# A transformer kernel on one core: the first weight chunk of each dense stage is split in four pieces among the last row blocks

## The chip, the core and the metric

The kernel runs on one NeuronCore of a Trainium2 chip. The core has a matrix engine (TensorE), three engines for elementwise work (VectorE, ScalarE, GpSimd), and SyncE, whose queue issues DMAs. Each engine runs its own list of instructions in order, and they meet at semaphores: an engine waits until a semaphore has reached a number, and finished instructions raise it. The metric is the device time of one execution in microseconds (us), as the median of several runs; lower is better.

## The reference

The program is two transformer blocks over 512 tokens of width 1024, in float32. The first has a mixer (mLSTM heads and a gated MLP), cross attention to 256 memory rows and a mixture of 32 experts; the second, run twice, has a token mixer with four branches and another mixture of experts. What matters here are the dense products in between. Cut to these:

```python
z = h @ w_in                                             # mixer: 1024 -> 3088 columns
x = x + jnp.concatenate([y_mlstm, y_gmlp], -1) @ w_out    # its output projection
q = h @ w_q;  kv = hm @ w_kv                              # cross attention
x = x + o @ w_o
z = x @ w_in                                             # token mixer, per layer
merged @ w_o                                             # its output projection, per layer
```

## The kernel before

Every dense product goes through `dense` (line 86). Its inputs are the activations, turned so that the 1024 features lie on the partitions (`hT`, 8 row blocks of 128 features by 512 tokens), and weight chunks of 256 columns or so (8 row blocks by 256 columns, 1 MB). To keep float32 accuracy at the fast rate, each operand is held as two float32r parts: HI is the rounded value, LO what is left. A product of one row block is three matmuls, HI x HI, HI x LO and LO x HI (`PARTS`), so one output item of `dense` is 8 x 3 = 24 matmuls into one PSUM bank.

A chunk is split in two steps. `high` (line 143, the copy on 147) casts the whole chunk to HI on ScalarE once its DMA has landed; `low` (line 161, line 164) subtracts that from the raw chunk on VectorE. A chunk has 2048 columns per partition, so these are long instructions. TensorE (lines 127 to 139) waits for `low_ready` of the item's chunk, then runs its 24 matmuls on line 137. Two split chunks are held, and two or three raw ones (`raw_ring`); SyncE loads chunk after chunk on line 124.

`before` is the helper that makes `hT` inside the same stage. `TurnSplit` (line 229): TensorE turns four 128x128 tiles into each of the eight PSUM banks (line 246), ScalarE writes HI of each row block (line 253), VectorE writes LO (line 261, or line 263 where a gain is applied). `Split` (line 267) does the same from SBUF without TensorE (lines 281 and 287). All three engines do all of `before` first and only then chunk 0:

```python
before.pe(pe)
pe.wait_ge(before.low_ready, before.n)     # all eight row blocks
...
before.act(act)                            # ScalarE: eight row blocks, then
high(0)                                    #   the whole of chunk 0
...
before.dve(dve)                            # VectorE: eight row blocks, then
low(0)
```

Eight stages call `dense` with a `before`. Four start with items of 512 columns, where the weights are the stationary operand (`by_feature`): mixw (the mixer's input, with a gain, `raw_ring` 2), xaw (cross attention, with a gain), t0w and t1w (the token mixer's input, layer 0 and 1). Four are output projections through `project_onto` (line 1526), with items of 256 columns (`by_token`): mixo, xao, t0o and t1o; of these t0o and t1o use `Split`, the others `TurnSplit`. Chunk 0 has two items in the first four and four in the projections. In mixw, t0w and t1w VectorE also has convolution taps as side work, behind the items of chunks 1 and later. Each stage ends in a clear of its semaphores and a barrier of all engines (lines 53 and 54).

Of the kernel before, what the change touches and what calls it, by code (L numbers as in the profile page):

```python
# [11 lines left out]
HI, LO = 0, 1  # L12
I32 = mybir.dt.int32
U32 = mybir.dt.uint32
ACT = mybir.ActivationFunctionType
# [65 lines left out]


WIDTH = 256


def dense(nc, name, k, chunks, items, raw_ring=3, side=None, before=None):

    ps = k["ps"]
    widest = max(c.shape[2] for c in chunks)
    deepest = max(c.shape[1] for c in chunks)
    last_item = {it.chunk: i for i, it in enumerate(items)}
    nth, counts = [], {"act": 0, "dve": 0}
    for it in items:
        counts[it.engine] += 1
        nth.append(counts[it.engine])
    with Stage(nc, name) as st:  # L100
        raw = st.sb("raw", [P, raw_ring, deepest, widest])
        w = st.sb("w", [P, 2, 2, deepest, widest], F32R)
        landed = [st.sem(f"weights_landed{i}") for i in range(raw_ring)]
        high_ready = st.sem("high_ready")
        low_ready = st.sem("low_ready")
        bank_full = st.sem("bank_full")
        emptied = {"act": st.sem("emptied_by_act"), "dve": st.sem("emptied_by_dve")}

        def raw_of(c):
            return raw[:, c % raw_ring, 0:chunks[c].shape[1], 0:chunks[c].shape[2]]  # L110

        def part_of(c, part):
            return w[:, c % 2, part, 0:chunks[c].shape[1], 0:chunks[c].shape[2]]

        if before is not None:
            before.begin(st)

        with nc.Block() as block:
            @block.sync
            def _(sp):  # L120
                for c, dram in enumerate(chunks):
                    if c >= raw_ring:
                        sp.wait_ge(low_ready, c - raw_ring + 1)
                    sp.dma_start(raw_of(c), dram).then_inc(landed[c % raw_ring], 16)

            @block.tensor
            def _(pe):
                if before is not None:
                    before.pe(pe)
                    pe.wait_ge(before.low_ready, before.n)  # L130
                for i, it in enumerate(items):
                    pe.wait_ge(low_ready, it.chunk + 1)
                    if i >= 8:
                        pe.wait_ge(emptied[items[i - 8].engine], nth[i - 8])
                    pairs = it.operands(w[:, it.chunk % 2])
                    for j, (stationary, moving) in enumerate(pairs):
                        last = nc.tensor.matmul(ps[0:it.rows, i % 8, 0:it.n], stationary, moving,
                                                start=j == 0, stop=j == len(pairs) - 1)
                    last.then_inc(bank_full, 1)

            @block.scalar
            def _(act):
                def high(c):
                    act.wait_ge(landed[c % raw_ring], 16 * (c // raw_ring + 1))
                    if c >= 2:
                        act.wait_ge(bank_full, last_item[c - 2] + 1)
                    nc.scalar.copy(part_of(c, HI), raw_of(c)).then_inc(high_ready, 1)

                if before is not None:
                    before.act(act)  # L150
                high(0)
                for c in range(len(chunks)):
                    if c + 1 < len(chunks):
                        high(c + 1)
                    for i, it in enumerate(items):
                        if it.chunk == c and it.engine == "act":
                            act.wait_ge(bank_full, i + 1)
                            it.out(nc.scalar, ps[0:it.rows, i % 8, 0:it.n]).then_inc(emptied["act"], 1)

            @block.vector  # L160
            def _(dve):
                def low(c):
                    dve.wait_ge(high_ready, c + 1)
                    nc.vector.tensor_tensor(part_of(c, LO), raw_of(c), part_of(c, HI), ALU.subtract).then_inc(low_ready, 1)

                if before is not None:
                    before.dve(dve)
                low(0)
                for c in range(len(chunks)):
                    if c + 1 < len(chunks):  # L170
                        low(c + 1)
                    for i, it in enumerate(items):
                        if it.chunk == c and it.engine == "dve":
                            dve.wait_ge(bank_full, i + 1)
                            it.out(nc.vector, ps[0:it.rows, i % 8, 0:it.n]).then_inc(emptied["dve"], 1)
                    if side is not None:
                        side(dve, c, emptied)


def chunk_of(w_dram, a, b):  # L180
    return w_dram.rearrange("(c p) n -> p c n", p=P)[:, :, a:b]
# [3 lines left out]
PARTS = ((HI, HI), (HI, LO), (LO, HI))  # L185
# [43 lines left out]
class TurnSplit:  # L229
# [16 lines left out]
                last = self.nc.tensor.transpose(self.bank(c)[:, t * P:(t + 1) * P], self.src(t, c), self.k["ident"][:])  # L246
            last.then_inc(self.full, 1)

    def act(self, act):
        for c in range(self.n):  # L250
            act.wait_ge(self.full, c + 1)
            scale = 1.0 if self.factor is None else self.factor[:, c:c + 1]
            self.nc.scalar.activation(self.dst[:, HI, c, :], self.bank(c), ACT.Identity, scale=scale).then_inc(self.high_ready, 1)

    def dve(self, dve):
        vec = self.nc.vector
        for c in range(self.n):
            dve.wait_ge(self.high_ready, c + 1)
            low, high = self.dst[:, LO, c, :], self.dst[:, HI, c, :]
            if self.factor is None:  # L260
                vec.tensor_tensor(low, self.bank(c), high, ALU.subtract).then_inc(self.low_ready, 1)
            else:
                vec.scalar_tensor_tensor(low, self.bank(c), self.factor[:, c:c + 1], high, ALU.mult,
                                         ALU.subtract).then_inc(self.low_ready, 1)


class Split:
# [8 lines left out]
    def pe(self, pe):  # L276
        pass

    def act(self, act):
        for c in range(self.n):  # L280
            self.nc.scalar.activation(self.dst[:, HI, c, :], self.src[:, c, :], ACT.Identity,
                                      scale=self.factor).then_inc(self.high_ready, 1)

    def dve(self, dve):
        for c in range(self.n):
            dve.wait_ge(self.high_ready, c + 1)
            self.nc.vector.scalar_tensor_tensor(self.dst[:, LO, c, :], self.src[:, c, :], self.factor,
                                                self.dst[:, HI, c, :], ALU.mult, ALU.subtract).then_inc(self.low_ready, 1)


def turn_split(nc, name, k, tiles, src, dst, n, factor=None):

    turned = TurnSplit(nc, k, tiles, src, dst, n, factor)
    with Stage(nc, name) as st:
        turned.begin(st)
        with nc.Block() as block:
            @block.tensor
            def _(pe):
                turned.pe(pe)

            @block.scalar
            def _(act):
                turned.act(act)

            @block.vector
            def _(dve):
                turned.dve(dve)


def plain(nc, out, gain=None):  # L310
# [1040 lines left out]
def mixer_one(nc, k, x, col, i):  # L1351
# [3 lines left out]
    with Stage(nc, "mix") as sx:  # L1355
# [5 lines left out]
        with Stage(nc, "mixa") as sa:  # L1361
# [6 lines left out]

            spans = [(a, a + WIDTH) for a in range(0, 1536, WIDTH)] + [(1536, 1800), (1800, 2064)]
            spans += [(a, a + WIDTH) for a in range(2064, 3088, WIDTH)]  # L1370
            chunks = [chunk_of(w, a, b) for a, b in spans]
# [5 lines left out]
            for c in range(2):  # L1377
                cs = slice(c * WIDTH, (c + 1) * WIDTH)
                for t in range(TT):
                    items.append(by_token(4 + c, hT, t, 0, WIDTH, "dve", plain(nc, v[:, t, cs])))  # L1380
            def output_gates(t, a):
# [474 lines left out]
class GatedBranches:  # L1856
# [78 lines left out]
    def high(self, act, u):  # L1935
        act.wait_ge(self.landed[u % self.RAW], 32 * (u // self.RAW + 1))
        if u >= self.SPLIT:
            act.wait_ge(self.proj_full, u - self.SPLIT + 1)
        self.nc.scalar.copy(self.w[:, u % self.SPLIT, HI], self.raw[:, u % self.RAW]).then_inc(self.high_ready, 1)

    def low(self, dve, u):
        dve.wait_ge(self.high_ready, u + 1)
        self.nc.vector.tensor_tensor(self.w[:, u % self.SPLIT, LO], self.raw[:, u % self.RAW],  # L1943
                                     self.w[:, u % self.SPLIT, HI], ALU.subtract).then_inc(self.low_ready, 1)
# [264 lines left out]
```

## Time and profile before

| | |
|---|---|
| three runs | 3113.94, 3120.40 and 3122.73 us, median 3120.4 |
| profiled execution | 3114.51 us, span in the profile 3112.7 us |
| TensorE matmuls | busy 2482.1 us, 80% of the span |
| TensorE weight loads | 1949.6 us, 63% |
| VectorE | 1284.4 us, 41% |
| ScalarE | 881.6 us, 28% |
| GpSimd | 406.1 us, 13% |
| DMA | 565.77 MB, 182 GB/s on average |
| TensorE's mean granted clock | 0.89 |

The shares are averages over stages with quite different limits: the expert stages stream their weights at up to 414 GB/s, while the dense stages move little and are full of matmuls. A dense stage has to be read by itself, in order of time. Times in the rows below are microseconds from the span's start; PE is the matmul side of TensorE and PEld its weight loads, DVE is VectorE, ACT ScalarE, SPq the issuing queue of SyncE. A row of a timeline gives start, length, engine, line and operation, the output and input tiles, how many instructions were merged, and in brackets how long the engine idled before and who ended it.

### The profile page before, as it was taken

The page shows a single profiled execution, that of the slowest core. Times are in us where ns is not written, and L with a number is a line of the kernel's source. Part 1 is how long each engine was busy: PE and PEld are TensorE (multiplying, and loading weights), DVE is VectorE, ACT ScalarE, POOL GpSimd, SP SyncE. Part 2 cuts the span into 40 slices and gives each one's busy share as a digit, 9 for nine tenths or more (in the row PEclk, how much of TensorE's full clock was granted, in tenths as well). Part 3 has the DMA queues.
Part 4 walks back from the last instruction along what each step waited for, and adds up shares of the span by engine and source line. Part 5 has one row for each costly group of instructions (what it writes and reads, how often), then busy time and mean ns, then how long its engine had stood idle before and what let it go on. Part 6 is the DMA issues. An engine that isn't in the chain of part 4 may idle for free. (4 is left out here: it accounts for less than half of the span.)

```text
span 3112.7 us, 50456 instructions
## 1 busy us (share of the span) xinstructions
PE 2482.1 (80%) x18120; PEld 1949.6 (63%) x18121; DVE 1284.4 (41%) x2666; ACT 881.6 (28%) x1612; POOL 406.1 (13%) x716
## 2 busy tenths in 40 slices
PE   4975798868888886969899669983959989849882
PEld 3964678844444445847677657762848667747661
DVE  3437345232111115634653434335644744343334
ACT  2233234111111112144532213322233632213221
POOL 0000000022111210000000124432000000024333
PEclk9988899879999997979999869996979999959996
DMA  3200242389999954122121378994212212179993
GB/s 114 93 1 1 68 135 75 158 322 404 407 414 410 390 239 138 41 68 60 43 68 43 121 286 339 384 367 135 69 35 68 60 51 68 55 288 346 378 393 136
DMA packets 209256, 565.77 MB, mean 182 GB/s; under 512 B 26550, under 2 KB 170550, under 8 KB 184544
## 3 DMA queue, kind: packets, MB, share of 16 engines
q1 hardware_dynamic: 191056, 538.71, 46.7%
q0 software_dynamic: 18064, 25.23, 2.5%
q8 instruction: 87, 1.43, 0.2%
q14 instruction: 49, 0.40, 0.0%
HBM read 560.44 MB, written 36.18 MB: 192 GB/s over the span
## 5 line engine op out<-in xcount | busy, mean ns | idle before, releaser
L1020 PEld LDWEIGHTS ps<-r_gate_up,e_xT 128*64 128x64 f32 x2272 | 267.0, 144 | 92.3 <-issue 88.8
L1020 PE MATMUL ps<-m_gate_up,e_xT 128*64 128x256 f32 x1088 | 269.7, 411 | 61.9 <-DMA m_gate_up<-in_w_gate_up 48.0
L1020 PE MATMUL ps<-r_gate_up,e_xT 128*64 128x128 f32 x2272 | 279.1, 284 | 43.0 <-DMA r_gate_up<-in_w_exp_gate_up 28.5
L1022 PE MATMUL ps<-r_gate_up,e_xT 128*64 128x128 f32 x2272 | 279.3, 284 | 0.0
L1022 PE MATMUL ps<-m_gate_up,e_xT 128*64 128x256 f32 x1088 | 269.8, 411 | 0.0
L1020 PEld LDWEIGHTS ps<-m_gate_up,e_xT 128*64 128x64 f32 x1088 | 159.8, 149 | 174.2 <-issue 110.3
L1022 PEld LDWEIGHTS ps<-r_gate_up,e_xT 128*64 128x64 f32 x2272 | 267.0, 144 | 0.0
L1174 DVE TENSOR_TENSOR e_hid<-e_silu,ps 64x128 f32<-64x128 f32 (+1 forms) x210 | 70.1, 335 | 472.7 <-ACT e_silu L1062 467.9
L1062 ACT ACTIVATE e_silu<-ps 64x128 f32<-64x128 f32 (+1 forms) x210 | 63.8, 304 | 641.8 <-PE ps L1022 641.8
L455 POOL TENSOR_TENSOR all_x<-all_x,ln_rows 128x1024 f32<-128x1024 f32 x16 | 48.2, 3038 | 1263.7 <-DVE all_x L448 1263.7
L1921 PE MATMUL ps<-t_hT,t0a_t0g_w 128*128 128x512 f32 x768 | 199.4, 411 | 4.6 <-DVE t0a_t0g_w L1943 2.4
L1921 PE MATMUL ps<-t_hT,t1a_t1g_w 128*128 128x512 f32 x768 | 199.2, 411 | 4.6 <-DVE t1a_t1g_w L1943 2.4
L1180 DVE TENSOR_SCALAR e_y<-ps 128x512 f32 x105 | 72.6, 692 | 248.9 <-PE ps L1037 213.3
L1921 PEld LDWEIGHTS ps<-t_hT,t0a_t0g_w 128*128 128x128 f32 x768 | 145.5, 194 | 45.8 <-issue 10.3
L1921 PEld LDWEIGHTS ps<-t_hT,t1a_t1g_w 128*128 128x128 f32 x768 | 145.3, 194 | 45.7 <-issue 10.3
L1062 ACT ACT_TABLE_LOAD x105 | 134.7, 1283 | 124.0 <-issue 114.2
L1022 PEld LDWEIGHTS ps<-m_gate_up,e_xT 128*64 128x64 f32 x1088 | 159.8, 149 | 0.0
L1037 PE MATMUL ps<-r_down,e_hidT 128*64 128x512 f32 x568 | 137.5, 605 | 0.0
L1218 POOL COPY e_choicecur<-e_choicecol 128x1 uint32 x106 | 52.3, 493 | 588.5 <-DVE e_y L1180 588.5
L1213 POOL DMA_INDIRECT e_landing<-e_dram_rows,e_tokcur x115 | 117.0, 1017 | 59.5 <-issue 59.5
L1037 PE MATMUL ps<-m_down,e_hidT 128*64 128x512 f32 x544 | 124.2, 598 | 0.0
L1221 POOL DMA_INDIRECT e_dram_y<-e_y,e_choicecur x106 | 110.4, 1041 | 56.4 <-issue 56.0
(605 smaller groups left out, 4740.1 us busy)
## 6 DMA issues: line engine op xcount, KB each, us to landing
m_gate_up<-in_w_gate_up SPq DMA_DIRECT2D x32, 4096.0 KB, 38.2
r_gate_up<-in_w_exp_gate_up SPq DMA_DIRECT2D x64, 2048.0 KB, 33.8
m_down<-in_w_down SPq DMA_DIRECT2D x32, 2048.0 KB, 37.9
r_down<-in_w_exp_down SPq DMA_DIRECT2D x64, 1024.0 KB, 34.7
t0a_t0g_raw<-in_w_in SPq DMA_DIRECT2D x32, 512.0 KB, 3.8
t1a_t1g_raw<-in_w_in SPq DMA_DIRECT2D x32, 512.0 KB, 3.8
mixw_raw<-in_w_in SPq DMA_DIRECT2D x10, 1024.0 KB, 5.4
xaw_raw<-in_w_kv_x SPq DMA_DIRECT2D x8, 1024.0 KB, 5.3
```

Of the source, the lines that this page charges most:

```text
L455: nc.gpsimd.tensor_tensor(x[:, t, :], x[:, t, :], rows[:, 1], ALU.add).then_inc(shifted, 1)
L1020: nc.tensor.matmul(ps_gu[q][0:SLOTS], xT[:, c, :], ring.gu[:, s, 0, c, span], start=c == 0, stop=c == DC - 1)
L1022: last = nc.tensor.matmul(ps_gu[q][SLOTS:P], xT[:, c, :], ring.gu[:, s, 1, c, span], start=c == 0, stop=c == DC - 1)
L1037: last = nc.tensor.matmul(ps_y[h * SLOTS:(h + 1) * SLOTS], hidT[:, f, :], ring.wd[:, s, f, h * 512:(h + 1) * 512], start=f == 0, stop=f == ...
L1062: nc.scalar.activation(silu[SLOTS:P, q], ps_gu[q][0:SLOTS], ACT.Silu).then_inc(silu_ready, 1)
L1174: vec.tensor_tensor(hid[SLOTS:P, q], silu[SLOTS:P, q], ps_gu[q][SLOTS:P], ALU.mult).then_inc(hid_ready, 1)
L1180: vec.tensor_scalar(y[:, bass.ds(g % 2, 1)].rearrange("p one d -> p (one d)"), ps_y, 1.0, None, ALU.mult).then_inc(y_copied, 1)
L1213: nc.gpsimd.indirect_dma_start(landing[:, p], None, rows_dram, bass.IndirectOffsetOnAxis(tokcur[p][:], 0), bounds_check=S - 1, oob_is_err= ...
L1218: nc.gpsimd.tensor_copy(choicecur[p][:], choicecol[:, bass.ds(n, 1)]).then_inc(choicecur_ready, 1)
L1221: nc.gpsimd.indirect_dma_start(y_dram, bass.IndirectOffsetOnAxis(choicecur[p][:], 0), y[:, p], None, bounds_check=4 * S - 1, oob_is_err=Fa ...
L1921: last = nc.tensor.matmul(ps[:, 6, :], w[:, p, q, :], self.hT[:, r, q, :], start=q == 0 and p == r, stop=q == DC - 1 and p == LO)
```

## The change

For stages with a `before`, chunk 0 is split in `FIRST` = 4 pieces of two row blocks (512 columns per partition). ScalarE writes HI of row blocks 0 to 4, waits for chunk 0's landing, casts piece 0, then writes block 5, piece 1, block 6, piece 2, block 7, piece 3. VectorE follows in the same order with the LO parts. Pieces have semaphores of their own, `first_high_ready` and `first_low_ready`, and `low_ready` now counts from chunk 1 on. On TensorE the wait for all eight row blocks is gone; inside item 0, ahead of the three matmuls of row block q, stands a wait for row block q's LO and, for every second q, one for the piece. Item 1 and later ones of chunk 0 wait for all four pieces. The helpers' loops over row blocks (`act`, `dve`) become one call for each block (`high`, `low`), which `turn_split` now loops over itself. Nothing that is computed changes.

```diff
+FIRST = 4
@@ dense
+    first = FIRST if before is not None else 1
+    step = chunks[0].shape[1] // first
+        first_high_ready = st.sem("first_high_ready")
+        first_low_ready = st.sem("first_low_ready")
+        def wait_low(engine, c):
+            if c == 0:
+                engine.wait_ge(first_low_ready, first)
+            else:
+                engine.wait_ge(low_ready, c)
@@ SyncE
-                        sp.wait_ge(low_ready, c - raw_ring + 1)
+                        wait_low(sp, c - raw_ring)
@@ TensorE
-                    pe.wait_ge(before.low_ready, before.n)
-                    pe.wait_ge(low_ready, it.chunk + 1)
+                    if i > 0 or before is None:
+                        wait_low(pe, it.chunk)
                     for j, (stationary, moving) in enumerate(pairs):
+                        if i == 0 and before is not None and j % len(PARTS) == 0:
+                            q = j // len(PARTS)
+                            pe.wait_ge(before.low_ready, q + 1)
+                            if q % step == 0:
+                                pe.wait_ge(first_low_ready, q // step + 1)
@@ ScalarE
+                def first_high(n):
+                    if n == 0:
+                        act.wait_ge(landed[0], 16)
+                    span = slice(n * step, (n + 1) * step)
+                    nc.scalar.copy(part_of(0, HI)[:, span], raw_of(0)[:, span]).then_inc(first_high_ready, 1)
-                    before.act(act)
-                high(0)
+                    for c in range(before.n):
+                        before.high(act, c)
+                        if c >= before.n - first:
+                            first_high(c - before.n + first)
+                else:
+                    first_high(0)
@@ VectorE
+                def first_low(n):
+                    dve.wait_ge(first_high_ready, n + 1)
+                    span = slice(n * step, (n + 1) * step)
+                    nc.vector.tensor_tensor(part_of(0, LO)[:, span], raw_of(0)[:, span], part_of(0, HI)[:, span],
+                                            ALU.subtract).then_inc(first_low_ready, 1)
-                    before.dve(dve)
-                low(0)
+                    for c in range(before.n):
+                        before.low(dve, c)
+                        if c >= before.n - first:
+                            first_low(c - before.n + first)
+                else:
+                    first_low(0)
```

## Rows read from the trace of the kernel before

**Rows 1.** Line 164 asked by source: who waited for it (us, times)
```profile
  PE ps L137: 56.8, 8
```

**Rows 2.** Timeline, opening of mixw
```profile
35.60 13.60 SPq L124 DMA_DIRECT2D mixw_raw<-in_w_in  x4
...
35.64 5.70 PE L246 MATMUL ps<-all_ident,mix_y 128*128 128x128 f32 x32 [35.64 <-PEq L54]
...
37.48 6.03 DVE L263 SCALAR_TENSOR_TENSOR mix_hT<-ps,all_columns,mix_hT 128x512 fp32r<-128x512 f32 x8 [2.58 <-ACT mix_hT L253]
...
39.32 3.17 ACT L253 ACTIVATE mix_hT<-ps,all_columns 128x512 fp32r<-128x512 f32 x5 [0.17 <-PE ps L246]
...
46.75 5.43 PE L137 MATMUL ps<-mix_hT,mixw_w 128*128 128x512 f32 x16 [5.41 <-DVE mixw_w L164]
```

**Rows 3.** Timeline, opening of t0o
```profile
1712.69 4.27 ACT L281 ACTIVATE t_hT<-t_merged 128x512 fp32r<-128x512 f32 x8 [2.93 <-PEq L54]
1713.36 4.91 DVE L287 SCALAR_TENSOR_TENSOR t_hT<-t_merged,t_hT 128x512 fp32r<-128x512 f32 x8 [1.41 <-ACT t_hT L281]
1717.84 1.90 ACT L147 CAST t0o_w<-t0o_raw 128x2048 fp32r<-128x2048 f32 x1 [0.88 <-DMA t0o_raw<-in_w_o]
1719.77 2.29 DVE L164 TENSOR_TENSOR t0o_w<-t0o_raw,t0o_w 128x2048 fp32r<-128x2048 f32 x1 [1.51 <-ACT t0o_w L147]
...
1722.21 5.96 PE L137 MATMUL ps<-t0o_w,t_hT 128*128 128x256 f32 x34 [11.79 <-DVE t0o_w L164]
```

**Rows 4.** DMA issues, chunk 0 of four stages: issue, queue, count, size, us to landing
```profile
mixw_raw<-in_w_in SPq DMA_DIRECT2D x1, 1024.0 KB, 6.0
...
xaw_raw<-in_w_q_x SPq DMA_DIRECT2D x1, 1024.0 KB, 5.1
...
t0w_raw<-in_w_in SPq DMA_DIRECT2D x1, 1024.0 KB, 5.2
...
t1w_raw<-in_w_in SPq DMA_DIRECT2D x1, 1024.0 KB, 5.3
```

**Rows 5.** Timeline, TensorE's transposes and first products in xaw, t0w and t1w
```profile
394.11 5.66 PE L246 MATMUL ps<-all_ident,xa_h 128*128 128x128 f32 x32 [1.75 <-PEq L54]
...
405.18 2.05 PE L137 MATMUL ps<-xa_hT,xaw_w 128*128 128x512 f32 x4 [5.41 <-DVE xaw_w L164]
...
1191.46 6.33 PE L246 MATMUL ps<-all_ident,all_x 128*128 128x128 f32 x32 [32.84 <-PEq L54]
...
1202.73 3.75 PE L137 MATMUL ps<-t_hT,t0w_w 128*128 128x512 f32 x8 [4.94 <-DVE t0w_w L164]
...
2155.57 5.57 PE L246 MATMUL ps<-all_ident,all_x 128*128 128x128 f32 x32 [43.85 <-PEq L54]
...
2166.19 4.12 PE L137 MATMUL ps<-t_hT,t1w_w 128*128 128x512 f32 x10 [5.05 <-DVE t1w_w L164]
```

**Rows 6.** Groups by line and form: count | busy, mean ns | idle before, releaser
```profile
L137 PE MATMUL ps<-t0o_w,t_hT 128*128 128x256 f32 x384 | 48.0, 289 | 11.8 <-DVE t0o_w L164 11.8
...
L137 PE MATMUL ps<-mix_hT,mixw_w 128*128 128x512 f32 x192 | 46.2, 403 | 5.4 <-DVE mixw_w L164 5.4
```

**Rows 7.** Windows, first 10 us of products; after the five engines, PEclk, DMA share, GB/s
```profile
46.75:56.75 10.00, 10.00 (x37) 8.06 (x38) 2.79 (x4) 0.00 (x0) 0.00 (x0) 0.84 0.65 211
...
405.18:415.18 10.00, 10.00 (x37) 8.15 (x38) 2.75 (x2) 0.00 (x0) 0.00 (x0) 0.84 0.68 211
...
1202.73:1212.73 10.00, 10.00 (x35) 7.97 (x36) 2.75 (x2) 0.00 (x0) 0.00 (x0) 0.78 0.58 170
...
2166.19:2176.19 10.00, 10.00 (x37) 8.00 (x38) 2.75 (x2) 0.00 (x0) 0.00 (x0) 0.83 0.58 172
```

**Rows 8.** Timeline and windows around xao's transposes (end 535.60) and product (541.87)
```profile
531.91 3.69 PE L246 MATMUL ps<-all_ident,xa_h 128*128 128x128 f32 x32 [1.50 <-PEq L54]
...
529.00:531.91 2.91, 1.42 (x8) 0.94 (x6) 1.29 (x4) 0.00 (x1) 0.00 (x0) 1.00 0.00 0
...
535.60:538.94 3.34, 0.00 (x0) 0.00 (x0) 2.48 (x5) 2.43 (x4) 0.00 (x0) 0.88 1.10 352
```

More of the change, by code:

```diff
@@ L161, in _ @@
             def _(dve):
+                def first_low(n):
[3 more added lines that the diff above has]
+                                            ALU.subtract).then_inc(first_low_ready, 1)
                 def low(c):
-                    dve.wait_ge(high_ready, c + 1)
+                    dve.wait_ge(high_ready, c)
                     nc.vector.tensor_tensor(part_of(c, LO), raw_of(c), part_of(c, HI), ALU.subtract).then_inc(low_ready, 1)
                 if before is not None:
-                    before.dve(dve)
-                low(0)
+                    for c in range(before.n):
[4 more added lines that the diff above has]
+                    first_low(0)
                 for c in range(len(chunks)):
@@ L247, in pe, with high, low @@
             last.then_inc(self.full, 1)
[L249 to L255, printed above, removed]
-        vec = self.nc.vector
[L257 to L264, printed above, removed]
+    def high(self, act, c):
+        act.wait_ge(self.full, c + 1)
+        scale = 1.0 if self.factor is None else self.factor[:, c:c + 1]
+        self.nc.scalar.activation(self.dst[:, HI, c, :], self.bank(c), ACT.Identity, scale=scale).then_inc(self.high_ready, 1)
+    def low(self, dve, c):
+        vec = self.nc.vector
+        dve.wait_ge(self.high_ready, c + 1)
+        low, high = self.dst[:, LO, c, :], self.dst[:, HI, c, :]
+        if self.factor is None:
+            vec.tensor_tensor(low, self.bank(c), high, ALU.subtract).then_inc(self.low_ready, 1)
+        else:
+            vec.scalar_tensor_tensor(low, self.bank(c), self.factor[:, c:c + 1], high, ALU.mult,
+                                     ALU.subtract).then_inc(self.low_ready, 1)
 class Split:
@@ L277, in pe, with high, low @@
         pass
[L279 to L288, printed above, removed]
+    def high(self, act, c):
+        self.nc.scalar.activation(self.dst[:, HI, c, :], self.src[:, c, :], ACT.Identity,
+                                  scale=self.factor).then_inc(self.high_ready, 1)
+    def low(self, dve, c):
+        dve.wait_ge(self.high_ready, c + 1)
+        self.nc.vector.scalar_tensor_tensor(self.dst[:, LO, c, :], self.src[:, c, :], self.factor,
+                                            self.dst[:, HI, c, :], ALU.mult, ALU.subtract).then_inc(self.low_ready, 1)
 def turn_split(nc, name, k, tiles, src, dst, n, factor=None):
@@ L302, in _ @@
             def _(act):
-                turned.act(act)
+                for c in range(n):
+                    turned.high(act, c)
             @block.vector
             def _(dve):
-                turned.dve(dve)
+                for c in range(n):
+                    turned.low(dve, c)
 def plain(nc, out, gain=None):
```

## The prediction, made before the changed kernel was run

> **What bounds the kernel now.** I read the page first, for which engine is busy, and then, because the change lives only in `dense`, the waits that line 137 (the products) has there. In the whole run those products wait eight times for line 164, the float32 remainder of a weight chunk, once in each of the eight dense stages, for 56.8 us together [rows 1]. No later chunk is waited for in this way, so behind its first product each stage runs at TensorE's pace, and whatever brings product 25 (the second item) forward brings the end of the stage forward. So I read the opening of the stages in order of time: who is late there?
>
> In mixw, one of the four stages with 512-column products, the transposes end at 41.34, ScalarE's row blocks at 42.49, VectorE's at 43.51, and the first product starts only at 46.75 [rows 2]. Between lies the whole of chunk 0: cast and then subtraction, one behind the other. In t0o, one of the four output projections (256 columns), ScalarE is done with its blocks at 1716.96 and then idles 0.88 us for chunk 0's landing; cast 1.90, subtraction 2.29, product at 1722.21 [rows 3]. The serial chain is landing (or last block), 1.90, 2.29, 0.15.
>
> **The change, part by part.**
>
> *Splitting.* One cast of 2048 columns becomes four of 512. For ScalarE the nearest row is the same width from SBUF in t0o: 0.61 for one, and eight in 4.27, so one each 0.52 us; for VectorE 0.69, eight in 4.91, one each 0.60 [rows 3]. Four pieces cost about 2.2 us against 1.90 and 2.5 against 2.29. From below: 0.48 and 0.57 a piece, the exact quarter; from above 0.69, the longest 512-column row of ScalarE [rows 2], and 0.75 on VectorE. I take 0.60 and 0.62. This is 0.2 to 0.3 us per stage and engine, and it lies beside products, see below.
>
> *Order.* ScalarE now does blocks 0 to 4, waits for chunk 0, then piece 0, block 5, piece 1, block 6, piece 2, block 7, piece 3; VectorE follows in the same order. The wait for the landing thus moves ahead of three row blocks, and queued behind it on ScalarE are those blocks, behind them VectorE's remainders, and TensorE. Landing after issue is 6.0, 5.1, 5.2 and 5.3 us in mixw, xaw, t0w and t1w [rows 4]. Block 4's cast in mixw ends about 40.8 (the second of five from 39.32 [rows 2]), so ScalarE stands 0.8 us; in t0o block 4 ends at 1715.4 and it stands 2.4 us until 1717.84 [rows 3]. That delays blocks 5 to 7, yet not the first product, which now needs only row block 0 and piece 0.
>
> *First product.* It comes at landing + 0.60 + 0.03 + 0.69 + 0.15 = landing + 1.47. mixw: 35.60 + 6.0 + 1.47 = 43.07 against 46.75, 3.7 us earlier. xaw: 394.07 + 5.1 + 1.47, with 0.1 for VectorE's block 4 still running, 400.75 against 405.18, 4.4. t0w: 1191.41 + 5.2 + 1.47 = 1198.1 against 1202.73, 4.6. t1w: 2155.53 + 5.3 + 1.47 = 2162.3 against 2166.19, 3.9 [rows 2, 4, 5] (the issue is 0.04 to 0.05 before the first transpose). Sum 16.6. t0o: 1717.84 + 1.47 = 1719.3 against 1722.21, 2.9 [rows 3]; mixo, xao and t1o have the same chain from landing to product (a landing wait, then 1.90, 2.29), so four times 2.9 = 11.7. Together 28.3 us.
>
> *Do the products keep up, or do they now wait for pieces?* VectorE gives a piece and a block each 0.60 + 0.62 = 1.22 us (1.3 in mixw and xaw, whose blocks take 0.66 to 0.75 [rows 2]). Six products use one piece and two blocks. The 192 wide products of mixw take 46.2 us, 0.24 each, so six take 1.4 at full clock: TensorE stays the slower one, and the shift passes whole to the second item. Narrow ones take 48.0/384 = 0.125 [rows 6], six 0.75 at full clock and twice that, 1.5, at half. Those stages begin at half clock (below), so there too TensorE paces. If they ran at full clock they would be held by the last piece: first product + 3 x 1.22 + 0.15 + 0.75, 4.6 us for the item, no longer than they need when they warm up on the way. Last piece lands about 0.7 us later than the last subtraction did; chunk 1 behind it is ready 1 us later, and is needed no sooner than 48 wide or 96 narrow products after the start, 11 us: hidden.
>
> *Waits.* Twelve waits inside item 0 (eight for blocks, four for pieces). The trace shows only what an unsatisfied one costs, 0.15 us from VectorE's end to the product [rows 3], and that one was there before. I take 0 for the others, since they are fulfilled when TensorE comes to them; the other end is 0.15 at each of seven later boundaries, 8 us over eight stages. Two more semaphores per stage are in a clear that stands between barriers; no row of mine prices it, between 0 and 0.1 us a stage. Nothing else is moved: the SP queue issues the same loads, and only the load that reuses chunk 0's buffer waits for piece 3 in place of the whole, 0.7 us later with 10 us to spare.
>
> *Clock.* Now the products open each stage at 1.2 GHz: mean granted clock over their first 10 us is 0.84, 0.84, 0.78 and 0.83 in mixw, xaw, t0w and t1w [rows 7]. As the two levels are 0.5 and 1, the low stretch is 3.2, 3.2, 4.4 and 3.4 us, and half of it is lost: 7.1 us. In these four the clock was full when the transposes ended (TensorE idled 5.4 us and found 0.5). After the change it idles from 41.34 to 43.07 in mixw, 1.7 us, and about 1.0, 0.3 and 1.2 in xaw, t0w and t1w [rows 2, 5]. Before xao TensorE idles 1.50 us and the granted clock stays 1.00 across it [rows 8]. So I take the four low stretches as gone, 7.1 us, with 0 as the other end. In xao the transposes end at 535.60 and the product moves from 541.87 to 538.94; over that stretch the mean is already 0.88 [rows 8], so it has fallen before the product comes. In t0o TensorE has nothing to do before. I take the four projections to open at half clock as now, no gain.
>
> The Trainium skill, "TensorE: Matmul & The Clock Gate", § A second HAM failure mode: psum-queue depth-cycling, says that short idles between groups of products can make the clock swing between its levels. That speaks against this change, whose item 0 comes in groups of six. The row beside it, a 1.50 us idle at 1.00 [rows 8], does not show it; by the rule the 7.1 us would not come and some of the 28.3 would go.
>
> **Sum.** 28.3 + 7.1 = 35.4 us. The profiled execution took 3114.5 us around a span of 3112.7 and lies 5.9 below the median of 3120.4. It gives 3079 by itself; against the median 3085, which I forecast.
>
> **The rivals.**
>
> A, forecast: start earlier and clock kept: 3085, on its own 3076 to 3091 (profiled base; waits and clears at their upper ends).
>
> B, the shift comes but not the clock: the 1.7 us gap, or the wait at a group's end, finds TensorE at 1.2 GHz. For: in all eight stages TensorE opens low. Against: the idle of 1.50 us at 1.00 [rows 8]. 3120.4 - 28.3 = 3092; one or two stages of four lie between.
>
> C, item 0 runs in groups of six with a short idle after each, and the clock falls and stays low through it. (The Trainium skill's rule above leads here.) 24 wide products at 0.43 (512 columns at 1.2 GHz) are 10.2 us against the 7.1 that they take now in mixw (16 in 5.4, eight more at 0.24, less the last one's tail [rows 2]), so the shift of 4.2 shrinks to about 1.2 a stage, and the narrow ones to about 2.4: some 15 us left, 3105.
>
> D, slower: the low clock lasts over item 1 too. Its place is the product after item 0, its price half of each further low microsecond. It turns the sign where the eight stages together lose C's 15 us, that is with 3.8 us more of low clock in each. If all of item 1 is low, 4.7 us go in a wide stage and 2.3 in a narrow one, 28 us: 3120 - 15 + 28 = 3133. Against it: behind a start the clock rises within 3.2 to 4.4 us of steady work in these rows.
>
> E, the change does not do what it says, or half: a stage behind gives part back, or landing comes later once blocks wait on it, or each of the boundaries costs 0.15 to 0.25 us. 3120 - 18 = 3102. Against: landing does not depend on the engines' order, and no stage waits on a fixed time.
>
> **How the numbers follow.** A 0.55, B 0.22, E 0.08, C 0.11, D 0.04. I predict A, 3085. Range: A from the low base, 3074, over B to E, 3102; C and D and a little of A's lower end are left out, under 0.2. A measurement of this kernel can tell about 0.3%, 9.4 us, from no change. A, B, E and half of C gain more: 0.90. The rest of C and the weak half of D: 0.06. Slower: 0.04.
>
> **What would show it.** Four 512-column casts among the row blocks; TensorE's wait ahead of the first product 1.7 us in mixw, about 1.0 in xaw and 0.3 in t0w in place of 5.4 or so, 3.3 in xao, 8.9 in t0o in place of 11.8; the sum of waits for line 164's successor down by 28; granted clock 1.00 over the first 10 us in the four wide stages; first cast of chunk 1 about 1 us later. Wrong if item 0 shows a wait at each group of six, if granted clock in the wide stages is below 0.84, if ScalarE's landing wait exceeds 2.4 us, or if a stage behind grows.

## The result

The changed kernel takes 3078.4 us (median of four runs, 3075.83 to 3084.31), the kernel before 3118.1 beside it; the ratio is 0.9879 with a 95% interval of 0.9866 to 0.9893, so 1.2% faster. A second set of runs gave the same ratio (below). The profiled execution took 3084.31 us, the highest of the four, and that of before 3114.51, near the low end of its runs (3113.94 to 3122.73); so the spans of the two profiles lie only 30.1 us apart where the medians lie 40 apart.

| | before | after |
|---|---|---|
| span of the profiled execution | 3112.7 us | 3082.6 us |
| TensorE matmuls busy | 2482.1 us | 2473.0 us |
| ScalarE busy | 881.6 us | 882.2 us |
| VectorE busy | 1284.4 us | 1283.7 us |
| mean granted clock | 0.89 | 0.896 |
| wait of the first products, eight stages | 56.8 us [rows 1] | 33.8 us |

The page of the changed kernel: the span is 30.1 us shorter, and the busy times hardly move (TensorE's products 9.1 us less, its weight loads 10.9 less, the other engines within 1.6).

```profile
span 3082.6 us, 50528 instructions
PE 2473.0 (80%) x18120; PEld 1938.7 (63%) x18121; DVE 1283.7 (42%) x2690; ACT 882.2 (29%) x1636; POOL 407.7 (13%) x716
```

The products are on line 153 now, the pieces' casts on 163 and their subtractions on 191. The idle time of the products asked by source (us, times), where [rows 1] had the sum and [rows 6] two of the eight:

```profile
  DVE t1o_w L191: 8.9, 1
  DVE t0o_w L191: 8.8, 1
  DVE mixo_w L191: 4.3, 1
  DVE xao_w L191: 3.4, 1
  DVE xaw_w L191: 2.9, 1
  DVE mixw_w L191: 2.1, 1
  DVE t1w_w L191: 1.9, 1
  DVE t0w_w L191: 1.4, 1
...
  PE ps L153: 33.8, 8
```

Only one wait per stage, the one before the very first product, is left; none stands behind a group of six. The sum of the waits fell by 23.0 us and not by the 28 of the prediction's list of signs, although the first products came 27.7 us earlier (below), as the transposes ended earlier too, by 4.7 us in sum. The opening of mixw, where [rows 2] had the first product at 46.75:

```profile
35.67 14.26 SPq L135 DMA_DIRECT2D mixw_raw<-in_w_in  x4
...
35.71 5.12 PE L282 MATMUL ps<-all_ident,mix_y 128*128 128x128 f32 x32 [35.71 <-PEq L54]
...
41.50 0.62 ACT L163 CAST mixw_w<-mixw_raw 128x512 fp32r<-128x512 f32 x1 [1.11 <-DMA mixw_raw<-in_w_in]
...
42.15 0.69 DVE L191 TENSOR_TENSOR mixw_w<-mixw_raw,mixw_w 128x512 fp32r<-128x512 f32 x1 [0.81 <-ACT mixw_w L163]
...
42.98 9.29 PE L153 MATMUL ps<-mix_hT,mixw_w 128*128 128x512 f32 x39 [2.15 <-DVE mixw_w L191]
```

Landing at 41.50, then 0.62, 0.69 and 0.14: the product comes 1.48 us after the landing, at 42.98, 7.31 after the issue where it was 11.15 before. Measured in this way, from the stage's first load to its first product, the eight stages are 3.8 (mixw), 4.4 (xaw), 4.6 (t0w), 2.6 (t1w), 3.6 (mixo), 2.9 (xao), 3.0 (t0o) and 2.8 us (t1o) earlier, 27.7 together; at the last product of each stage it is 29.7. The remaining 0.4 of the 30.1 lies between the stages.

### The profile page after: what moved, and what is told of

Read it like the earlier page. It is cut to its first block and busy times, and to the rows that moved or that the text cites. A ratio compares the mean times of both kernels' runs of the same rounds, so it can differ in the third digit from the quotient of the medians.

```text
span 3082.6 us, 50528 instructions
## 1 busy us (share of the span) xinstructions
PE 2473.0 (80%) x18120; PEld 1938.7 (63%) x18121; DVE 1283.7 (42%) x2690; ACT 882.2 (29%) x1636; POOL 407.7 (13%) x716
```

## The experiments

All runs are set against the kernel before on the same chip. "Opening" is the time from a stage's first load to its first product.

**The waits alone.** The piece count is set to 1: products wait row block by row block, the chunk is one piece behind all blocks.

```diff
-FIRST = 4
+FIRST = 1
```

> Only the block-by-block waits: chunk 0 is one piece behind all row blocks (piece count 1). Theory: the whole chunk is the last thing to be ready, so the waits for single row blocks open nothing: within 0.1% of the kernel before, 3118, first products within 0.1 us of where they were. Rival (the waits for all row blocks held item 0): several us faster. It also prices the eight extra waits of item 0: under 1 us in all.

3115.0 us against 3114.2, ratio 0.9999 (0.9989 to 1.0009). The wait of the first products is where it was in [rows 1]:

```profile
  PE ps L153: 58.2, 8
```

So the fine waits win nothing alone, and also cost nothing: item 0 has nine waits here where it had two, and seven more in each of eight stages cannot be seen. The 0 that the prediction took for them was right, and its upper end of 8 us lies outside the interval. The first products did not stay within 0.1 us, as had been expected: the single stages moved by up to 0.9 us earlier (t0w) and 0.6 later (mixw, xaw), 0.7 later in sum. That is how far openings differ between two profiles when nothing is won.

**The pieces alone.** Four pieces among the blocks, but item 0 waits for everything.

```diff
                     before.pe(pe)
+                    pe.wait_ge(before.low_ready, before.n)
 ...
-                    if i > 0 or before is None:
-                        wait_low(pe, it.chunk)
+                    wait_low(pe, it.chunk)
```

> The changed kernel (four pieces among the row blocks), but item 0 waits for all row blocks and all pieces, as before. Theory (the gain is the earlier first product): the last piece lands 0 to 0.6 us later per stage than the whole chunk's subtraction did, so the gain is gone: within 3 us of the kernel before, 3115 to 3124 us, and TensorE's eight waits before its first products are back at about 57 to 60 us. Rival (the reordered ScalarE and VectorE work itself shortens the stages): most of the 38 us stays, about 3085.

3112.5 us, ratio 0.9991 (0.9981 to 1.0001): no gain either, and the waits are back, 5 us longer than before (62.1, where 57 to 60 were expected).

```profile
  PE ps L148: 62.1, 8
```

Neither half does anything without the other. The gain is the earlier first product, and it needs a small first piece and a wait for that piece only.

**Pieces, but behind the last block.**

```diff
                     for c in range(before.n):
                         before.high(act, c)
-                        if c >= before.n - first:
-                            first_high(c - before.n + first)
+                    for n in range(first):
+                        first_high(n)
```

and the same on VectorE.

> Four pieces and waits as in the changed kernel, but all pieces stand behind the last row block on ScalarE and VectorE, not among them. Theory: in the four projections the landing is last and nothing moves; in mixw, xaw, t0w and t1w the first product comes 1.2 to 2 us later than in the changed kernel. Sum about 5 to 6 us: 3084, against 3078 for the changed kernel. Rival (laying them among the blocks is what brings the gain): back above 3100.

3084.2 us, ratio 0.9899 (0.9881 to 0.9916). The wait of the first products:

```profile
  PE ps L153: 37.4, 8
```

The openings are 23.3 us shorter in sum, against 27.7: the four projections as in the changed kernel (2.6 to 3.7 us), the wide stages 0.6 to 1.7 less (1.2 to 2 were expected; xaw and t1w stayed below that). So of about 38 us some 32 come from the pieces and their waits, and about 6 (0.2%, with intervals that overlap) from laying them among the blocks.

**Two pieces instead of four.**

> The changed kernel with two pieces of 1024 columns instead of four. Theory (first product = landing + cast of a piece + subtraction of a piece): a piece takes about 1.0 and 1.2 us instead of 0.6 and 0.7, so each first product is 0.9 us later, 7 us in all, about 3085, unless a stage keeps its clock. Rival (the landing alone decides, the size of the piece is hidden): 3078.

3094.4 us, ratio 0.9925 (0.9908 to 0.9943). The direction is right, and so is the size for the openings: they are 19.2 us shorter in sum, 8.5 less than with four pieces, where 7 were expected. The time lost more, some 14 us by the two ratios. TensorE still waits only once in each stage:

```profile
  PE ps L153: 40.3, 8
```

so the longer piece 1 costs no wait of its own. What differs behind the openings is the granted clock: over the first 10 us it is 0.71 to 0.73 in the four projections, where the changed kernel has 0.75 to 0.84, and 0.83 and 0.84 in mixw and t1w. The second items are 20.4 us earlier (29.3 with four pieces), the last products 20.3 (29.7). So 9.4 of the 14 us show at the last products of the two profiles; where the rest lies no run says.

**The changed kernel once more.**

> The changed kernel once more, for its ratio from more runs and for a second profile. The first pair of profiles differs by 30 us and the first medians by 40. Theory (that difference is chance in which stages open at full clock and in landing times): ratio 0.988 to 0.990, first products again about 28 us earlier in sum, but another set of stages that open at full clock. Rival (something of 8 to 10 us lies outside the eight openings): the profile would show it between the stages.

3078.4 us, ratio 0.9879 (0.9863 to 0.9895), span of its profile 3075.6. The openings are 27.8 us shorter in sum, as in the first profile; but now all four wide stages open at full clock. Windows over the first 10 us of products; the third number from the right is the granted clock, as in [rows 7]. First the first profile of the changed kernel (mixw, xaw, t0w, t0o, t1w):

```profile
42.98:52.98 10.00, 9.99 (x43) 8.14 (x44) 6.58 (x10) 4.24 (x6) 0.00 (x0) 1.00 0.54 169
...
391.10:401.10 10.00, 10.00 (x32) 8.03 (x33) 6.62 (x8) 4.22 (x6) 0.00 (x0) 0.70 0.93 298
...
1182.19:1192.19 10.00, 10.00 (x43) 8.14 (x44) 6.35 (x8) 3.96 (x6) 0.00 (x0) 1.00 0.91 273
1695.94:1705.94 10.00, 9.99 (x65) 10.00 (x66) 6.51 (x9) 4.06 (x6) 0.00 (x0) 0.75 0.76 238
2140.85:2150.85 10.00, 10.00 (x37) 7.98 (x38) 6.44 (x8) 3.95 (x6) 0.00 (x0) 0.83 0.77 229
```

and the second (mixw, xaw, t0w, t1w):

```profile
42.91:52.91 10.00, 10.00 (x43) 8.15 (x44) 6.58 (x10) 4.23 (x6) 0.00 (x0) 1.00 0.57 182
...
391.32:401.32 10.00, 10.00 (x44) 8.30 (x45) 6.53 (x8) 4.23 (x6) 0.00 (x0) 1.00 0.94 296
...
1181.63:1191.63 10.00, 10.00 (x43) 8.15 (x44) 6.35 (x8) 3.95 (x6) 0.00 (x0) 1.00 0.90 272
...
2136.87:2146.87 10.00, 10.00 (x43) 8.15 (x44) 6.35 (x8) 3.96 (x6) 0.00 (x0) 1.00 0.76 225
```

At the stages' last products the sum is 33.5 us here, 3.8 more than in the first profile; the span differs from before by 37.1, so 3.6 lie between the stages, spread over them with both signs (-1.4 to +2.5). Part of the rival is therefore true, but that part is no single piece.

**TensorE kept at work in the gap.** After its transposes TensorE waits for row block 0 (so that bank 0 is free; t0o and t1o have no transposes and no such wait) and turns the identity 6 to 40 times.

```diff
                     before.pe(pe)
+                    if hasattr(before, "full"):
+                        pe.wait_ge(before.low_ready, 1)
+                    for _ in range(FILL[name]):
+                        nc.tensor.transpose(ps[:, 0, 0:P], k["ident"][:], k["ident"][:])
```

> The changed kernel, with TensorE kept at work in the gap before item 0: 6 to 40 extra 128x128 transposes of the identity into bank 0 per stage, whose result is overwritten. Theory (an idle TensorE is what brings the half clock): item 0 opens at 1.00 in xaw and t1w too, where the changed kernel lost 3.0 and 1.7 us, and in the projections, where little is to be had as item 0 is then held by its pieces: 4 to 6 us less, about 3073. Rival (the clock falls on its own, whatever TensorE did before): no change of the first 10 us' granted clock, 3078.

3080.0 us, ratio 0.9879 (0.9863 to 0.9896): no faster than the changed kernel on the same chip. But the clock did what the theory said: 1.00 over the first 10 us in seven of the eight stages, all but xao. Here mixo, xao and t0o:

```profile
314.85:324.85 10.00, 9.30 (x75) 8.77 (x74) 6.46 (x9) 3.90 (x6) 0.00 (x0) 1.00 0.55 182
...
524.05:534.05 10.00, 9.74 (x66) 9.36 (x67) 6.50 (x9) 3.94 (x6) 0.00 (x0) 0.83 0.57 182
...
1695.19:1705.19 10.00, 9.22 (x71) 8.70 (x72) 6.52 (x9) 4.06 (x6) 0.00 (x0) 1.00 0.71 228
```

The 4 to 6 us had been counted against the first profile, where xaw and t1w opened low; in the runs beside this one the changed kernel had full clock there already. In a projection full clock is worth little: t0o's second item comes 2.9 us earlier than before instead of 2.4, as item 0 is held by its pieces (TensorE 9.22 busy of 10 above, where it was 9.99 at the lower clock). And in this profile the openings are 24.8 us shorter instead of 27.8, mostly in xao (1.7 instead of 3.1) and t0w (3.2 instead of 4.6), where chunk 0 landed 1.4 us later than in the second profile of the changed kernel. So what the clock gave was of the size of what landings take and give from run to run.

**Chunk 0 also loaded in four pieces.**

```diff
-                    sp.dma_start(raw_of(c), dram).then_inc(landed[c % raw_ring], 16)
+                    if c == 0:
+                        for n in range(first):
+                            span = slice(n * step, (n + 1) * step)
+                            sp.dma_start(raw_of(0)[:, span], dram[:, span]).then_inc(piece_landed[n], 16)
+                    else:
+                        sp.dma_start(raw_of(c), dram).then_inc(landed[c % raw_ring], 16)
```

with each piece's cast waiting for its own landing.

> The changed kernel, with chunk 0 also loaded in four pieces (256 KB each, a semaphore each), so that piece 0 can be cast when it has landed. In the changed kernel ScalarE waits 15.1 us in eight stages for the landing of the whole chunk. Theory: what is late now is that landing; piece 0 lands 1.5 to 2.5 us sooner, and the first products come 0.5 (t0w) to 2.5 us (projections) sooner: 8 to 13 us less, 3066 to 3070. Rival (the small loads land hardly sooner, as they share their engines with the next chunks, or three more issues in front of chunk 1 cost as much): 3078 or more.

3065.3 us, ratio 0.9841 (0.9824 to 0.9857), and in another set 3069.7, 0.9853 (0.9834 to 0.9872). By the ratios that is 8 to 12 us below the changed kernel; the first set's interval lies clear of the changed kernel's (0.9866 to 0.9893), the second's just overlaps it. ScalarE's waits for chunk 0 (line 168 here) fell from 15.1 us in eight stages to 2.0 in three:

```profile
  DMA mixo_raw<-in_w_out: 1.5, 1
  DMA t1o_raw<-in_w_o: 0.3, 1
  DMA xao_raw<-in_w_o_x: 0.2, 1
```

The opening of t0o, where the first product was 9.54 us behind the load before and 6.56 in the changed kernel, and is 4.54 now:

```profile
1685.41 1.91 SPq L139 DMA_DIRECT2D t0o_raw<-in_w_o  x4
...
1688.11 0.62 ACT L168 CAST t0o_w<-t0o_raw 128x512 fp32r<-128x512 f32 x1
...
1689.95 7.29 PE L159 MATMUL ps<-t0o_w,t_hT 128*128 128x256 f32 x46 [6.78 <-DVE t0o_w L196]
```

The openings are 37.8 us shorter in sum, 10.1 more than in the changed kernel. The projections gained 1.8 to 2.2 us each; t0w gained 0.1 and not the 0.5 expected, since ScalarE no longer waits for a landing there and row block 4 comes last ahead of the first piece. A second effect came with it: TensorE idles only 0.3 to 1.4 us in mixw, xaw, xao, t0w and t1w, and all five open at 1.00.

**The same with filler in the projections.**

> Chunk 0 loaded in four pieces, and the filler transposes (6 to 20) only in the four projections, the stages that still lose 5.3 us to the half clock in the profile of the kernel with the loads in pieces. Theory: they open at full clock, and 1 to 4 us go: 3061 to 3064. Rival: the filler overruns the earlier landing and costs what it brings: 3065 or more.

3069.3 us, 0.9848 (0.9833 to 0.9864): no gain, the rival's number, but not by its mechanism. The filler did not overrun the landing, as TensorE still idled 0.8 to 1.2 us behind it. Mixo opened at 1.00 and its second item came 0.4 us sooner; t0o and t1o stayed at 0.82 with 20 extra transposes, and xao had been at 1.00 already.

**The pieces as early as they can be.** Piece n behind block 2n, with the loads in pieces.

```diff
-                        if c >= before.n - first:
-                            first_high(c - before.n + first)
+                        if c % step == 0:
+                            first_high(c // step)
```

and the same on VectorE.

> Chunk 0 loaded in four pieces, and the pieces laid as early as their blocks need them: piece 0 behind block 0, piece 1 behind block 2, piece 2 behind block 4, piece 3 behind block 6. In the kernel with the loads in pieces ScalarE hardly waits for chunk 0 any more, and the first product comes behind block 4. Theory: in the four wide stages TensorE's own transposes are then last, so the idle time left there (0.3 to 1.2 us each, 2.8 together) can go; in the projections the first product comes sooner but item 0 still ends with VectorE's twelve instructions, so nothing is won. 3062 to 3065. Rival (ScalarE now stands at block 0 for piece 0's landing, and all blocks and pieces come later by that): some 0.5 to 1 us lost per stage, 3068 to 3073.

3077.6 us, ratio 0.9870 (0.9853 to 0.9886), beside 0.9853 of the kernel with the late order on the same chip. First products come earliest of all, 44.6 us in sum, and yet this is no faster than the changed kernel. In the wide stages the second item comes 0.5 to 1.1 us sooner than with the late order. The loss is in the projections. t0o, timeline of TensorE:

```profile
1694.42 1.62 PE L159 MATMUL ps<-t0o_w,t_hT 128*128 128x256 f32 x6 [6.47 <-DVE t0o_w L196]
1696.23 1.62 PE L159 MATMUL ps<-t0o_w,t_hT 128*128 128x256 f32 x6 [0.18 <-DVE t0o_w L196]
1698.03 1.62 PE L159 MATMUL ps<-t0o_w,t_hT 128*128 128x256 f32 x6 [0.18 <-DVE t0o_w L196]
1699.84 0.55 PE L159 MATMUL ps<-t0o_w,t_hT 128*128 128x256 f32 x1 [0.18 <-DVE t0o_w L196]
```

Item 0 runs in groups of six, one each 1.8 us, and ahead of each TensorE waits for VectorE, which needs that time for a piece and two blocks. Product 25 comes 11.06 us after the load instead of 9.03: a start 0.3 us earlier has become 2.0 us later. Where VectorE's last remainder stands says why. ScalarE's first cast and VectorE's last instruction of the opening, here (the load is issued at 1690.20):

```profile
1692.93 0.62 ACT L168 CAST t0o_w<-t0o_raw 128x512 fp32r<-128x512 f32 x1 [2.08 <-DMA t0o_raw<-in_w_o]
...
1699.61 0.68 DVE L324 SCALAR_TENSOR_TENSOR t_hT<-t_merged,t_hT 128x512 fp32r<-128x512 f32 x1
```

and VectorE's last with the late order (load at 1685.41, first cast without a wait):

```profile
1692.73 0.69 DVE L196 TENSOR_TENSOR t0o_w<-t0o_raw,t0o_w 128x512 fp32r<-128x512 f32 x1
```

The last remainder ends 10.09 us after the load and not 8.01, 2.1 us later, and the end of item 0 needs it in either order. It is late because ScalarE stood 2.08 us at block 0 for piece 0's landing, with its other seven blocks queued behind and VectorE's work behind those. That is the rival that had been set against this run, dearer than it was priced (0.5 to 1 us a stage) and in the projections alone: there VectorE's last remainder is 1.9 to 2.1 us later, and product 25 is 1.3 us later in mixo and 1.9 to 2.0 in the others.

The clock comes on top. The granted clock over the first 10 us of t0o, here and then with the late order:

```profile
1694.42:1704.42 10.00, 9.45 (x49) 8.65 (x50) 8.50 (x12) 6.25 (x10) 0.00 (x0) 0.64 1.02 325
```

```profile
1689.95:1699.95 10.00, 10.00 (x70) 10.00 (x71) 6.17 (x9) 4.04 (x5) 0.00 (x0) 0.82 1.00 322
```

At 0.64 the low stretch is 7.2 us against 3.6, but most of it falls where TensorE waits for VectorE anyway. The clock's own price shows best in xao: two more microseconds are lost there between product 25 and the last product. The granted clock of xao, here and then with the late order:

```profile
519.50:529.50 10.00, 7.99 (x39) 7.10 (x40) 8.46 (x12) 6.00 (x10) 0.00 (x0) 0.73 0.99 320
```

```profile
519.62:529.62 10.00, 9.24 (x71) 8.71 (x72) 5.19 (x7) 3.93 (x5) 0.00 (x0) 1.00 0.95 302
```

At their last products the four projections lose 9.9 us against the late order; 7.2 of them are there at product 25. So this is only in part the prediction's rival C. The Trainium skill, "TensorE: Matmul & The Clock Gate", § A second HAM failure mode: psum-queue depth-cycling, says that short idles between groups of products can make the clock swing between its levels. Here the trace agrees in xao, where TensorE opened at 1.00, idled 0.67 us ahead of each later group and was down to half 4.6 us after its first product. It does not agree for every short idle: with the late order xao idles 0.25 to 0.26 us ahead of three groups and stays at 1.00 over its first 10 us, and so do mixo, t0o and t1o in the run with TensorE kept at work. No run separates the idles from what else the early order changes, so why the clock falls stays open.

**Early in the wide stages only.** One condition is added, so that the early order holds where the first item has 512 columns.

> The loads in pieces, with the pieces laid early only in mixw, xaw, t0w and t1w, and behind block 4 on in the four projections. With the early order everywhere the second item came 0.6 to 1.3 us sooner in the four wide stages than with the late order, and 1.5 to 2.1 us later in the projections, whose granted clock over the first 10 us fell to 0.63 to 0.73. Theory (the early start harms only where TensorE works in small groups with idle between): 3 to 5 us below the kernel with the late order everywhere, ratio 0.983 to 0.984, and the projections' clock is back at 0.82 and above. Rival (what the early order cost lies elsewhere): 0.985 to 0.987.

3067.3 us, ratio 0.9833 (0.9820 to 0.9847). The ratio is the expected one, but it cannot be told apart from the late order everywhere (0.9841 and 0.9853), and at the last products its profile is only 1.1 to 1.2 us ahead of the two with the late order. It shows that the harm lay in the projections, and not which of the two causes above did it, as both go with the early order. The wide stages kept their 1.00, and three projections were back at 0.81 to 1.00; t0o stood at 0.73, below the 0.82 that was expected.

## Why the prediction was right, and where it was not

*Forecast and time.* 3085 was forecast, 3078.4 came, a gain of 38 (0.0121 x 3118) against 35.4. That the total came so close is in part luck: at the last products of the eight stages the two profiles of the changed kernel gain 29.7 and 33.5 us, and what lies beyond that was not forecast.

*The bound.* Right: TensorE paces the stages, and one wait per stage was worth having. What the start won was there at the last product (27.7 at the first products, 29.7 at the last).

*First product at landing + 1.47.* Right: 1.48 to 1.49 us in all eight stages. Sum 28.3 predicted, 27.7 and 27.8 measured. Single stages differ by their landing alone: t1w was put at 3.9 and gave 2.6, since chunk 0 landed at 6.6 us and not at 5.3,

```profile
2132.78 14.74 SPq L135 DMA_DIRECT2D t1w_raw<-in_w_in  x5
...
2139.36 0.62 ACT L163 CAST t1w_w<-t1w_raw 128x512 fp32r<-128x512 f32 x1 [1.41 <-DMA t1w_raw<-in_w_in]
```

and mixo gave 3.6 for 2.9, as its chunk landed at 6.5 and not at 7.2. ScalarE's longest wait for a landing was 3.3 us (mixo), above the 2.4 that I had named as a sign of being wrong; mixo still gained 4.8 us at its last product.

*Products keep up with the pieces.* Right: no wait behind the first in any stage of the first profile, and one, of 0.26 us in xao, in the second. The last subtraction is not 0.7 us later everywhere: 0.6 to 0.8 in xao, t0o and t1o, 0 in mixo, 1.0 in t1w with its later landing, and 0.1 to 1.0 earlier in the other three.

*Price of the splitting and of the waits.* Piece casts of 0.60 to 0.63 and subtractions of 0.68 to 0.69 were taken at 0.60 and 0.69 in the time of the first product; in the paragraph on splitting VectorE's piece had been put at 0.62, and it takes 0.60 only from start to start. The waits cost nothing, by the run with one piece.

*The clock term.* This term was mis-sized, and the gaps that it went by did not hold. Four stages were to win 7.1 us. In the first profile mixw won 1.5 and t0w 2.0 beyond their start, xaw lost 1.3 and t1w nothing, 2.2 in all; in the second profile the four won 6.6. The gaps had been taken from the times of before's transposes [rows 2, 5]. Transposes too run at either clock: in xaw they took 5.66 us at mixed clock [rows 5] and 3.69 now,

```profile
384.47 3.69 PE L282 MATMUL ps<-all_ident,xa_h 128*128 128x128 f32 x32 [1.75 <-PEq L54]
...
391.10 9.19 PE L153 MATMUL ps<-xa_hT,xaw_w 128*128 128x512 f32 x27 [2.94 <-DVE xaw_w L191]
```

so they ended sooner while the landing did not, and the gap was 2.94 us and not 1.0. That the granted clock then opened at 0.5 cost 3.0 us (a mean of 0.70 over 10). So two of the prediction's own signs of being wrong came: xaw at 0.70 and t1w at 0.83 lie below its 0.84, beside ScalarE's wait of 3.3 us. The gap does not settle it alone, though: t1w opened low after 1.89 us in the first profile and at 1.00 after 2.72 in the second. In the projections a small loss was overlooked: t0o and t1o stayed at half clock for 4.8 to 5.0 us instead of 3.8 (a granted mean of 0.75 and 0.76 over the first 10 us, 0.81 in before), 0.5 us each. Why they stay low longer is open.

*Rivals.* A held, with part of B: B is what the first profile shows in xaw and t1w. C and D did not come in the changed kernel; the run with the earliest pieces shows groups with idle and a low clock, but its loss is for the most part VectorE's later end. E did not come: the landings ahead of the first casts are 0.5 us later in sum in either profile (t1w 1.3 later in both profiles, mixo 0.7 and 0.5 earlier), the waits are free, and the stretches between the stages give back nothing that has one sign. In the paragraph on how the numbers follow, the last two chances are added wrongly: half of C and half of D are 0.075 and not 0.06, and 0.02 is left for slower, not 0.04.

*The 8 to 10 us between profiles and medians.* The two profiles of the changed kernel differ by 7.0 us: 3.8 of it in the eight stages, where xaw and t1w opened at full clock in one and not in the other, and the rest between the stages. As the kernel before has one profile only, no run says how much of the remaining difference is its own chance.

## What to carry to other kernels

Where a pipeline's first product waits for a long serial preparation, cut the preparation in pieces and let the product wait for the first of them; either half alone gave nothing here (0.9991, 0.9999), both together 1.2%. Then ask what is last in the new chain: here it was the landing of the whole chunk, and cutting the load in the same pieces gave another 0.3 to 0.4%. Stop where an earlier place makes the producer stand: the start that was earliest of all was worth less than one that came later, because the engine that waited for the first piece had the rest of the work queued behind, and the first item needs the last piece as well as the first.

## What the runs showed of the hardware that I had not expected

How long TensorE idled before its first product does not by itself say at which clock the stage opens. By the mean granted clock over the first 10 us, the four wide stages of all the profiles above stood at 1.00 after every idle of 1.8 us or less, and below 1.00 after every idle above 3.2 us. In between they stood at 1.00 five times (after 2.15, 2.67, 2.72, 2.91 and 3.14 us) and below it six times (after 1.89, 2.42, 2.46, 2.58, 2.94 and 3.15 us); in two of the six, 1.89 and 3.15, the first product still ran at full clock, which fell 0.4 and 1.5 us later. A forecast can therefore put a chance on such a stage, and not a number.

Transposes run at either clock too: the same 32 took 5.66 us in xaw before, at mixed clock, and 3.69 in the changed kernel.

ScalarE loses little to being cut: each of the four casts of 512 columns takes 0.60 to 0.63 us, but the next instruction already starts 0.51 to 0.53 us after its start. Four such steps make 2.1 us, against 1.90 for the whole chunk in one cast.
